# Stick-breaking attention: scores of two heads on the two halves of the array's rows, and a new order of score, turn and gather

## The chip, the cores and the metric

One Trainium2 chip, one core of it. The metric is the device time of the whole program in microseconds (us), smaller is better. The kernel before takes 2886.84 us (median of three runs, 2885.94 to 2888.79). The profiled execution, from which all rows below come, took 2888.11 us and has a span of 2886.3 us from its first to its last instruction.

## The reference, cut to what matters

The reference is one decoder block over 2048 positions: an input projection, a state-space mixer, stick-breaking attention with 8 heads of 64 elements, an output product, cross attention, and an MLP. The change touches the stick-breaking attention alone:

```
logits = einsum('bqhd,bkhd->bhqk', q, k) * scale        # 64 elements per head
mask = key_pos < q_pos
log_beta = log_sigmoid(logits)
log_1m_beta = where(mask, log_sigmoid(-logits), 0)
after = reverse cumsum over keys of log_1m_beta, less log_1m_beta
w = where(mask, exp(log_beta + after), 0)
out = einsum('bhqk,bkhd->bqhd', w, v)
```

The kernel does it as products: sigmoid(z) times the running product of sigmoid(-z) over the keys behind it. All data are float32. q and k of each head lie in device memory as two parts of 64 rows, a rounded part (hi) and what the rounding left (lo), so that q = hi + lo and k = hi + lo.

## The kernel before, in words

`stick_breaking` works on two heads at a time, in four steps (s). Within a step there are 16 blocks of 128 query positions (i). A block's keys are all keys up to its own, in tiles of 128, and `attention_units` cuts them into units of 1 to 4 tiles (128 to 512 keys), from the last keys to the first. A slot is one unit of one head; the slots alternate between the two heads (a = 0, 1), so a pair of slots, even and odd, is the same unit of both heads. There are 4 x 40 x 2 = 320 slots, or 160 pairs. The first unit of each block (`first`) holds the diagonal tile and is masked there.

Each slot m goes through these hands, each engine in its own written order:

- **score(m)** on TensorE (lines 957 to 982). The stationary operand is q2, 128 rows: q's hi part on the upper 64, its lo part on the lower 64. Line 976 multiplies it with k2_hi (k's hi part, stored twice, on both halves of the rows) and line 977 with k2_lo (likewise). That is two products of 128 rows for each slot, four in all for a pair, each as wide as the unit; a unit that crosses key 1024 is cut there in two segments. Line 979 adds the mask on the diagonal tile. The result is in one of five PSUM banks (`z_ps`, ZS = 5). TensorE waits until slot m - 5, which had the bank before, was scanned.
- **sigmoids(m)** on ScalarE: line 886 writes sigmoid(z) to `on`, line 887 writes sigmoid(-z) over z.
- **scan(m)** on VectorE (line 921): the running product into `left`.
- **w(m)** on GpSimd (line 873): `on` times `left`. Ring of WS buffers.
- **turn(m)** on TensorE (line 991): one transpose for each tile, into one of two PSUM banks (`wt_ps`). It waits (line 988) until the bank's last user, the slot two before, was copied out.
- **copies(m)**: the transposed weights from PSUM to `wt`. Slots with m % 3 != 2 are copied by ScalarE (line 895), the others by VectorE (line 932). Every slot has at most four tiles, so a slot is one such group.
- **gather(m)** on TensorE for a pair (line 1010): values times weights, with 64 columns of the array for each of the two heads; each tile and head gives two instructions in the trace.
- **copy_y** on VectorE (line 943), once for two finished blocks.

The order on each engine is set by lags, in slots. TensorE's loop over m issues score(m + 4), then turn(m - 3), and after every second m gather(m - 8) for the pair m - 8, m - 7. ScalarE's loop issues sigmoids(m), then copies(m - 7). VectorE's issues copy_y(m - 9), copies(m - 5), scan(m). Nothing else orders them but semaphores. SyncE loads q, k and v a half step ahead, and stores the result.

Of the kernel before, what the change touches and what calls it, by code (L numbers as in the profile page):

```python
# [7 lines left out]
F32 = mybir.dt.float32  # L8
F32R = mybir.dt.float32r
# [6 lines left out]
P = 128  # L16
BANK = 512
D_MODEL = 1024
SEQ = 2048
# [5 lines left out]
HEAD = 64  # L25
# [10 lines left out]
DMA = 16  # L36
# [683 lines left out]
def stick_breaking(nc, q_dram, k_dram, v_dram, yt_dram, ahead):  # L720

    BLOCKS = SEQ // P
    HALF = SEQ // 2
# [4 lines left out]
    SLOTS = [(s, a, *u) for s in range(STEPS) for u in UNITS for a in range(2)]  # L728
    N = len(SLOTS)
    PER_STEP = N // STEPS  # L730
    ZS, ONS, WS, WTS = 5, 6, 6, 8
    LEAD, TURN_LAG, ACT_LAG, DVE_LAG, GATHER_LAG, Y_LAG = 4, 3, 7, 5, 7, 9
    with ExitStack() as ctx:
        def sb(name, shape, dt=F32):
            return ctx.enter_context(nc.sbuf_tensor("a_" + name, shape, dt))

        sem = ctx.enter_context(semaphores(nc, "a_"))

        q2 = [sb(f"q2_{a}", [P, SEQ], F32R) for a in range(2)]
        k2_hi = [[sb(f"k2_hi{a}{r}", [P, HALF], F32R) for r in range(3)] for a in range(2)]  # L740
        k2_lo = [[sb(f"k2_lo{a}{r}", [P, HALF], F32R) for r in range(3)] for a in range(2)]
        v = [[sb(f"v{a}{r}", [P, BLOCKS * HEAD // 2]) for r in range(3)] for a in range(2)]
        ident = sb("ident", [P, P])
        ident16 = sb("ident16", [P, P], BF16)
        never16 = sb("never16", [P, P], BF16)
# [6 lines left out]
        z_ps = [ctx.enter_context(nc.psum_tensor(f"a_ps_z{b}", [P, WIDE], F32)) for b in range(ZS)]  # L752
# [6 lines left out]
        q_loaded = [sem(f"q_loaded{h}") for h in range(2)]  # L759
        k_loaded = [sem(f"k_loaded{h}") for h in range(2)]  # L760
        v_loaded = [sem(f"v_loaded{h}") for h in range(2)]
        begin_loaded = [sem(f"begin_loaded{a}") for a in range(2)]
        y_stored = [sem(f"y_stored{part}") for part in range(4)]
        scored = sem("scored")
# [20 lines left out]
        def wait(eng, of, count):  # L785
            if count > 0:
                eng.wait_ge(of, count)
# [4 lines left out]
        def wait_copied(eng, g):  # L792

            wait(eng, copied_a, acts_before[g + 1])
            wait(eng, copied_d, g + 1 - acts_before[g + 1])

        def load_begin(eng, a, cols, done_q, done_k):

            eng.dma_start(q2[a][:, cols].bitcast(F32), q_dram[a, :, cols]).then_inc(done_q, DMA)
            for dst, part in ((k2_hi[a][0], 0), (k2_lo[a][0], 1)):  # L800
                for copy in range(2):
                    eng.dma_start(dst[copy * HEAD:(copy + 1) * HEAD, cols].bitcast(F32),
                                  k_dram[a, part * HEAD:(part + 1) * HEAD, cols]).then_inc(done_k, DMA)

        @block.sync
        def _(sp):
            def load_half(s, half):
                cols = slice(half * HALF, (half + 1) * HALF)
                r = (2 * s + half) % 3
                if s > 0:  # L810
                    scores_of_q = final_slot[(s - 1) * BLOCKS + (BLOCKS // 2 - 1 if half == 0 else BLOCKS - 1)] + 1
                    wait(sp, scored, scores_of_q)
                for a in range(2):
                    sp.dma_start(q2[a][:, cols].bitcast(F32), q_dram[2 * s + a, :, cols]).then_inc(q_loaded[half], DMA)
                step_out = s - 1 if half else s - 2
                wait(sp, scored, (step_out + 1) * PER_STEP)
                for a in range(2):
                    for dst, part in ((k2_hi[a][r], 0), (k2_lo[a][r], 1)):
                        for copy in range(2):
                            sp.dma_start(dst[copy * HEAD:(copy + 1) * HEAD, :].bitcast(F32),  # L820
                                         k_dram[2 * s + a, part * HEAD:(part + 1) * HEAD, cols]).then_inc(k_loaded[half], DMA)
                wait_gathered(sp, (step_out + 1) * PER_STEP)
                for a in range(2):
                    h = 2 * s + a
                    sp.dma_start(v[a][r][:, :].rearrange("p (i d) -> p i d", d=HEAD),
                                 v_dram[cols, h * HEAD:(h + 1) * HEAD].rearrange("(i p) d -> p i d", p=P)).then_inc(v_loaded[half], DMA)

            def store_half(s, half):
                for part in (2 * half, 2 * half + 1):
                    wait(sp, y_copied, (s * BLOCKS + (part + 1) * 4) // 2)  # L830
                    sp.dma_start(yt_dram[s * P:(s + 1) * P, part * BANK:(part + 1) * BANK], yt[:, part, :]
                                 ).then_inc(y_stored[part], DMA)

            load_begin(sp, 0, slice(0, BANK), begin_loaded[0], begin_loaded[0])
            for a in range(2):
                sp.dma_start(v[a][0][:, :].rearrange("p (i d) -> p i d", d=HEAD),
                             v_dram[0:HALF, a * HEAD:(a + 1) * HEAD].rearrange("(i p) d -> p i d", p=P)
                             ).then_inc(v_loaded[0], DMA)
            for a in range(2):
                load_begin(sp, a, slice(BANK, HALF), q_loaded[0], k_loaded[0])  # L840
            load_half(0, 1)
            ahead.load_first(sp, ahead_loaded)
            for s in range(STEPS):
                store_half(s, 0)
                if s + 1 < STEPS:
                    load_half(s + 1, 0)
                    load_half(s + 1, 1)
                else:
                    sp.wait_ge(y_stored[0], STEPS * DMA)
                    ahead.load_ys(sp, yt_dram, ahead_loaded)  # L850
                store_half(s, 1)
            sp.wait_ge(ahead_loaded, ahead.FIRST_LOADS * DMA)
            for part in range(4):
                sp.wait_ge(y_stored[part], STEPS * DMA)
# [99 lines left out]
        def _(pe):  # L954
            pe.wait_ge(constants, 5)

            def score(m):

                s, a, i, k0, k1, first, last = SLOTS[m]
                if s == 0 and i == 0:  # L960
                    pe.wait_ge(begin_loaded[a], 5 * DMA)
                elif i == (BANK // P if s == 0 else 0) or i == BLOCKS // 2 and first:
                    half = i // (BLOCKS // 2)
                    pe.wait_ge(q_loaded[half], (s + 1) * 2 * DMA)
                    pe.wait_ge(k_loaded[half], (s + 1) * 8 * DMA)
                wait(pe, scanned, m - ZS + 1)
                c0 = k0
                while c0 < k1:
                    c1 = min(c0 + BANK - (c0 - k0) % BANK, k1, (c0 // HALF + 1) * HALF)
                    r = (2 * s + c0 // HALF) % 3  # L970
                    cols = slice(c0 % HALF, c0 % HALF + c1 - c0)
                    out = z_ps[m % ZS][:, c0 - k0:c1 - k0]
                    diagonal = first and c1 == k1
                    opens = (c0 - k0) % BANK == 0
                    closes = c1 == k1 or (c1 - k0) % BANK == 0
                    pe.matmul(out, q2[a][:, i * P:(i + 1) * P], k2_hi[a][r][:, cols], start=opens, stop=False)  # L976
                    mm = pe.matmul(out, q2[a][:, i * P:(i + 1) * P], k2_lo[a][r][:, cols], start=False, stop=closes and not diagonal)
                    if diagonal:
                        mm = pe.matmul(z_ps[m % ZS][:, k1 - P - k0:k1 - k0], ident16[:, :], never16[:, :],  # L979
                                       start=False, stop=True)  # L980
                    c0 = c1
                mm.then_inc(scored, 1)

            def turn(m):
                pe.wait_ge(weighed, m + 1)
                for g in range(first_group[m], first_group[m + 1]):
                    _, t0, n = groups[g]
                    if g >= 2:
                        wait_copied(pe, g - 2)
                    for t in range(n):  # L990
                        mm = pe.transpose(wt_ps[g % 2][:, t * P:(t + 1) * P], w[m % WS][:, (t0 + t) * P:(t0 + t + 1) * P],  # L991
                                          ident[:, :])
                    mm.then_inc(turned, 1)
# [17 lines left out]
                                       wt[(m + a) % WTS][:, t, :], start=(first and t == 0), stop=(last and t == tiles - 1))  # L1011
                mm.then_inc(pairs_gathered, 1)

            for m in range(LEAD):
                score(m)
            for m in range(N + GATHER_LAG):
                if m + LEAD < N:
                    score(m + LEAD)
                if TURN_LAG <= m < N + TURN_LAG:
                    turn(m - TURN_LAG)  # L1020
                if m > GATHER_LAG and (m - GATHER_LAG) % 2:
                    gather(m - GATHER_LAG - 1)


def ssm_scan(nc, small, scan, u_dram, y_dram, mem, g_mem, w_kv, g_q, g_k, kt_dram, mv_dram):
# [1142 lines left out]
class UpInputs:  # L2168
# [4 lines left out]
    SLOTS = 4  # L2173
# [1244 lines left out]
```

## Time and profile before

| what | value |
|---|---|
| median of the runs | 2886.84 us |
| profiled execution: time, span | 2888.11 us, 2886.3 us |
| attention, first score product to last gather (within the span) | 596.5 us to 1040.4 us |
| of the whole span: PE, DVE, ACT, POOL busy | 94%, 64%, 47%, 32% |

PE is TensorE's matmuls, PEld its weight loads, DVE VectorE, ACT ScalarE, POOL GpSimd. Matmuls are pipelined: a row's duration goes on after the next one has started, so the cost of one is read from the difference of two starts, and not from its duration. The same holds in smaller measure for ACT, whose next instruction starts some 0.1 us before the last one's end.

### The profile page before, as it was taken

Reading aid. Unit: us, or ns where it says so; the run is one execution under the profiler, and the core shown is the slowest. Engines: PE = TensorE matmul, PEld = TensorE weight load, DVE = VectorE, ACT = ScalarE, POOL = GpSimd, SP = SyncE. Lnnn points to the kernel's source line nnn. Section 1 sums busy time; section 2 is a strip of 40 time slices with the busy share of each in tenths; the row PEclk is TensorE's granted clock in tenths of the full one; section 3 lists DMA queues with packets and bytes.
Section 4 is the critical chain, followed back from the end, with each engine's and each line's share of the span. In section 5 each row is a group of like instructions: output and inputs, shape, how many; then the busy total and the mean of one; then the engine's idle time right before and its main releaser. Section 6 shows DMA issues by size and latency. Waiting matters only on the chain. (4 is left out here: it accounts for less than half of the span.)

```text
span 2886.3 us, 43692 instructions
## 1 busy us (share of the span) xinstructions
PE 2721.2 (94%) x14835; PEld 2232.6 (77%) x14835; DVE 1854.6 (64%) x2821; ACT 1369.5 (47%) x2508; POOL 925.4 (32%) x839
## 2 busy tenths in 40 slices
PE   6999978979999989998999899999999999999998
PEld 5888874757777768876888688877888787878787
DVE  5343458958998975545666856565556758584853
ACT  4222225668888863323445555565555424242421
POOL 0010101746766732300000132242333344344442
PEclk9999988989999989998999999999999999999999
DMA  5433345283333133341322243325444465646554
GB/s 172 109 84 94 80 110 104 65 209 79 74 77 86 42 106 103 118 172 66 110 100 105 98 133 128 112 96 171 154 133 146 112 154 120 159 97 169 99 116 85
DMA packets 291144, 328.23 MB, mean 114 GB/s; under 512 B 113816, under 2 KB 220320, under 8 KB 290720
## 3 DMA queue, kind: packets, MB, share of 16 engines
q1 hardware_dynamic: 276704, 291.96, 33.9%
q0 software_dynamic: 13824, 33.56, 7.9%
q8 instruction: 83, 1.36, 0.2%
q10 hardware_dynamic: 464, 0.79, 0.1%
q14 instruction: 69, 0.57, 0.1%
HBM read 206.57 MB, written 126.88 MB: 116 GB/s over the span
## 5 line engine op out<-in xcount | busy, mean ns | idle before, releaser
L3329 PE MATMUL f_ps_bank<-f_big,h_wv 128*128 128x512 f32 x1280 | 503.2, 393 | 26.9 <-DVE f_big L3175 17.6
L3330 PE MATMUL f_ps_bank<-f_big,h_wv 128*128 128x512 f32 x1280 | 500.6, 391 | 0.0
L3331 PE MATMUL f_ps_bank<-f_big,h_wv 128*128 128x512 f32 x1280 | 500.3, 391 | 0.0
L873 POOL TENSOR_TENSOR a_w<-a_on,a_left 128x512 f32<-128x512 f32 (+3 forms) x320 | 304.2, 956 | 143.8 <-DVE a_left L921 131.8
L3015 POOL TENSOR_TENSOR h_w_sum<-w_raw 128x512 f32<-128x512 f32 x63 | 90.9, 1443 | 729.0 <-DMA w_raw<-in_w_up 453.4
L3072 ACT ACTIVATE h_wv<-h_w_sum 128x512 fp32r<-128x512 f32 x252 | 159.0, 631 | 345.7 <-PE f_ps_bank L3331 342.4
L3329 PEld LDWEIGHTS f_ps_bank<-f_big,h_wv 128*128 128x128 f32 x1280 | 241.7, 189 | 84.1 <-issue 28.9
L3331 PEld LDWEIGHTS f_ps_bank<-f_big,h_wv 128*128 128x128 f32 x1280 | 241.8, 189 | 50.7
L3171 DVE TENSOR_TENSOR h_wv<-w_raw,h_wv 128x512 fp32r<-128x512 f32 x189 | 177.9, 942 | 159.9 <-ACT h_wv L3072 155.8
L3330 PEld LDWEIGHTS f_ps_bank<-f_big,h_wv 128*128 128x128 f32 x1280 | 241.9, 189 | 49.8
L3072 ACT ACTIVATE h_wv<-w_raw 128x512 fp32r<-128x512 f32 x189 | 118.7, 630 | 198.0 <-PE f_ps_bank L3331 178.2
L921 DVE TENSOR_TENSOR_SCAN a_left<-a_ps_z,a_left,a_one 128x384 f32<-128x384 f32 (+2 forms) x192 | 202.6, 1096 | 0.0
L3330 PE MATMUL f_ps_bank<-hv_rest,h_wv 128*128 128x512 f32 x512 | 199.3, 389 | 0.0
L886 ACT ACTIVATE a_on<-a_ps_z 128x512 f32<-128x512 f32 (+3 forms) x320 | 171.0, 534 | 58.5 <-PE a_ps_z L979 35.9
L3171 DVE TENSOR_TENSOR h_wv<-h_w_sum,h_wv 128x512 fp32r<-128x512 f32 x252 | 186.1, 738 | 5.3 <-ACT h_wv L3072 1.5
L976 PE MATMUL a_ps_z<-a_k_hi,a_q 128*128 128x512 f32 (+3 forms) x368 | 155.2, 428 | 19.0 <-DMA a_k_lo<-k 14.5
L991 PE MATMUL a_ps_wt<-a_ident,a_w 128*128 128x128 f32 x1088 | 172.3, 274 | 0.2 <-DVE a_wt L932 0.2
L887 ACT ACTIVATE a_ps_z<-a_ps_z 128x512 f32<-128x512 f32 (+3 forms) x320 | 172.5, 539 | 0.0
L646 PE MATMUL p_acc<-p_w_hi,p_ht_hi 128*128 128x512 f32 x384 | 153.5, 400 | 3.6 <-DVE p_w_lo L542 3.6
L424 POOL TENSOR_TENSOR p_qn<-p_qn,p_gq_row 128x512 f32<-128x512 f32 x32 | 41.0, 1293 | 360.6 <-DVE p_qn L560 360.6
L1010 PE MATMUL a_ps_y<-a_wt,a_v 128*64 128x128 f32 x2176 | 153.7, 280 | 0.0
L648 PE MATMUL p_acc<-p_w_hi,p_ht_lo 128*128 128x512 f32 x384 | 151.0, 393 | 0.0
(430 smaller groups left out, 6323.3 us busy)
## 6 DMA issues: line engine op xcount, KB each, us to landing
w_raw<-in_w_up SPq DMA_DIRECT2D x32, 1024.0 KB, 6.7
a<-h_xr SPq DMA_DIRECT2D x128, 256.0 KB, 3.4
w_raw<-a SPq DMA_DIRECT2D x32, 1024.0 KB, 5.2
h_raw<-in_w_down SPq DMA_DIRECT2D x32, 512.0 KB, 6.6
out<-h_xr POOLq DMA_DIRECT2D x64, 256.0 KB, 4.4
out<-h_xr POOLq DMA_DIRECT2D x32, 512.0 KB, 5.6
early<-in_x SPq DMA_DIRECT2D x16, 512.0 KB, 4.6
q<-p_raw SPq DMA_DIRECT2D x64, 128.0 KB, 2.5
```

Source lines behind the costliest of these rows:

```text
L873: pool.tensor_tensor(w[m % WS][:, 0:k1 - k0], on[m % ONS][:, 0:k1 - k0], left[a][i % 2][:, at + k0 + 1:at + k1 + 1], ALU.mult).then_inc(we ...
L886: act.activation(on[m % ONS][:, 0:k1 - k0], z, ACT.Sigmoid, scale=SCALE).then_inc(sig_on, 1)
L887: act.activation(z, z, ACT.Sigmoid, scale=-SCALE).then_inc(sig_off, 1)
L921: dve.tensor_tensor_scan(left[a][i % 2][:, at + k0:at + k1][:, ::-1], z_ps[m % ZS][:, 0:k1 - k0][:, ::-1], one[:, 0:1].to_broadcast([P, k1 ...
L976: pe.matmul(out, q2[a][:, i * P:(i + 1) * P], k2_hi[a][r][:, cols], start=opens, stop=False)
L991: mm = pe.transpose(wt_ps[g % 2][:, t * P:(t + 1) * P], w[m % WS][:, (t0 + t) * P:(t0 + t + 1) * P], ident[:, :])
L1010: mm = pe.matmul(y_ps[a * HEAD:(a + 1) * HEAD, i % 2 * P:(i % 2 + 1) * P], v[a][(2 * s + half) % 3][:, cols], wt[(m + a) % WTS][:, t, :], ...
L3072: act.activation(wv(i, 0), W_SRC[i], ACT.Copy).then_inc(w_high.sem, 1)
L3171: dve.tensor_tensor(wv(i, 1), W_SRC[i], wv(i, 0).bitcast(F32), ALU.subtract).then_inc(w_low.sem, 1)
L3329: pe.matmul(o, wv(i, 0)[:, k, :], hv(i, 0)[:, k, :], start=(k == 0), stop=False)
L3330: pe.matmul(o, wv(i, 0)[:, k, :], hv(i, 1)[:, k, :], start=False, stop=False)
L3331: mm = pe.matmul(o, wv(i, 1)[:, k, :], hv(i, 0)[:, k, :], start=False, stop=(k == KH - 1))
```

## The change

q and k are stored once: `q_hi`, `q_lo`, `k_hi`, `k_lo` have head 0 on the upper 64 rows and head 1 on the lower 64. A score call is for a pair of slots. It makes three products for each head, hi x hi, lo x hi and hi x lo (the product lo x lo, which the kernel before had, is left out), each with 64 rows, the two heads' in turn, into two PSUM banks. The lags and the rings of buffers are changed, and gathers come for two pairs in a row.

```
-    ZS, ONS, WS, WTS = 5, 6, 6, 8
-    LEAD, TURN_LAG, ACT_LAG, DVE_LAG, GATHER_LAG, Y_LAG = 4, 3, 7, 5, 7, 9
+    ZS, ONS, WS, WTS = 5, 6, 8, 12
+    LEAD, TURN_LAG, ACT_LAG, DVE_LAG, GATHER_LAG, Y_LAG = 4, 4, 8, 6, 11, 11
+    BATCH = 4
...
-        q2 = [sb(f"q2_{a}", [P, SEQ], F32R) for a in range(2)]
-        k2_hi = [[sb(f"k2_hi{a}{r}", [P, HALF], F32R) for r in range(3)] for a in range(2)]
-        k2_lo = [[sb(f"k2_lo{a}{r}", [P, HALF], F32R) for r in range(3)] for a in range(2)]
+        q_hi, q_lo = [sb(f"q_{part}", [P, SEQ], F32R) for part in ("hi", "lo")]
+        k_hi, k_lo = [[sb(f"k_{part}{r}", [P, HALF], F32R) for r in range(3)] for part in ("hi", "lo")]
...
+        def load_q(eng, step, a, cols, done):
+            for part, dst in enumerate((q_hi, q_lo)):
+                eng.dma_start(dst[a * HEAD:(a + 1) * HEAD, cols].bitcast(F32),
+                              q_dram[2 * step + a, part * HEAD:(part + 1) * HEAD, cols]).then_inc(done, DMA)
+        def load_k(eng, step, a, r, to, cols, done):
+            for part, dst in enumerate((k_hi[r], k_lo[r])):
+                eng.dma_start(dst[a * HEAD:(a + 1) * HEAD, to].bitcast(F32),
+                              k_dram[2 * step + a, part * HEAD:(part + 1) * HEAD, cols]).then_inc(done, DMA)
...
-                wait(pe, scanned, m - ZS + 1)
+                wait(pe, scanned, m + 1 - ZS + 1)
+                rows = slice(i * P, (i + 1) * P)
+                bank = [z_ps[(m + a) % ZS] for a in range(2)]
+                ends = [(c0, c1) for c0, c1 in ((k0, min(k1, HALF)), (max(k0, HALF), k1)) if c0 < c1]
+                for c0, c1 in ends:
...
-                    pe.matmul(out, q2[a][:, i * P:(i + 1) * P], k2_hi[a][r][:, cols], start=opens, stop=False)
-                    mm = pe.matmul(out, q2[a][:, i * P:(i + 1) * P], k2_lo[a][r][:, cols], start=False, stop=closes and not diagonal)
...
+                    terms = ((q_hi, k_hi[r]), (q_lo, k_hi[r]), (q_hi, k_lo[r]))
+                    for n, (q, k) in enumerate(terms):
+                        for a in range(2):
+                            head = slice(a * HEAD, (a + 1) * HEAD)
+                            mm = pe.matmul(bank[a][:, c0 - k0:c1 - k0], q[head, rows], k[head, cols],
+                                           start=(c0 == k0 and n == 0), stop=(c1 == k1 and n == 2 and not first))
+                            if c1 == k1 and n == 2 and not first:
+                                mm.then_inc(scored, 1)
+                if first:
+                    for a in range(2):
+                        pe.matmul(bank[a][:, k1 - P - k0:k1 - k0], ident16[:, :], never16[:, :],
+                                  start=False, stop=True).then_inc(scored, 1)
...
-            for m in range(LEAD):
+            for m in range(0, LEAD, 2):
                 score(m)
-            for m in range(N + GATHER_LAG):
+            for m in range(0, N + GATHER_LAG + 1, 2):
                 if m + LEAD < N:
                     score(m + LEAD)
-                if TURN_LAG <= m < N + TURN_LAG:
-                    turn(m - TURN_LAG)
-                if m > GATHER_LAG and (m - GATHER_LAG) % 2:
-                    gather(m - GATHER_LAG - 1)
+                if 0 <= m + 1 - TURN_LAG < N:
+                    turn(m + 1 - TURN_LAG)
+                if 0 <= m + 2 - TURN_LAG < N:
+                    turn(m + 2 - TURN_LAG)
+                done = m + 1 - GATHER_LAG
+                if 0 <= done < N and done % BATCH == 0:
+                    for n in range(done, done + BATCH, 2):
+                        gather(n)
```

So TensorE's loop over even m is now: score of slots m + 4 and m + 5, turn(m - 3), turn(m - 2), and in every second round the gathers of slots m - 10 to m - 7. ScalarE's order is sigmoids(m), copies(m - 8); VectorE's is copy_y(m - 11), copies(m - 6), scan(m). The number of q and k transfers for a half step falls from 2 of 128 rows and 8 of 64 rows to 8 of 64 rows.

## Rows read from the trace of the kernel before

**Rows 1.** Busy time by stage: PE, PEld, DVE, ACT, POOL, clock, DMA share, GB/s.
```profile
620.00:1020.00 400.00, 400.00 (x3799) 317.35 (x3799) 360.60 (x422) 354.47 (x786) 280.52 (x294) 1.00 0.32 82
```
**Rows 2.** Waits from 620 to 1020 us: total us, times, longest.
```profile
DVE a_wt L932 <- PE a_ps_wt L991: 25.4, 34, 2.2
ACT a_on L886 <- PE a_ps_z L979: 23.7, 47, 1.0
ACT a_on L886 <- PE a_ps_z L977: 19.0, 47, 0.7
```
**Rows 3.** TensorE's matmuls in order: start us, us (from start to last end), what.
```profile
904.77 0.34 PE L977 MATMUL a_ps_z<-a_k_lo,a_q 128*128 128x384 f32 x1
...
905.85 0.60 PE L991 MATMUL a_ps_wt<-a_ident,a_w 128*128 128x128 f32 x4
906.38 1.09 PE L1010 MATMUL a_ps_y<-a_wt,a_v 128*64 128x128 f32 x16
907.40 0.50 PE L976 MATMUL a_ps_z<-a_k_hi,a_q 128*128 128x512 f32 x1
907.73 0.40 PE L977 MATMUL a_ps_z<-a_k_lo,a_q 128*128 128x512 f32 x1
907.97 0.49 PE L991 MATMUL a_ps_wt<-a_ident,a_w 128*128 128x128 f32 x3
...
908.48 0.34 PE L977 MATMUL a_ps_z<-a_k_lo,a_q 128*128 128x384 f32 x1
908.65 0.49 PE L991 MATMUL a_ps_wt<-a_ident,a_w 128*128 128x128 f32 x3
909.07 0.88 PE L1010 MATMUL a_ps_y<-a_wt,a_v 128*64 128x128 f32 x12
909.88 0.44 PE L976 MATMUL a_ps_z<-a_k_hi,a_q 128*128 128x384 f32 x1
```
**Rows 4.** TensorE's weight loads in the same stretch.
```profile
907.40 0.19 PEld L976 LDWEIGHTS a_ps_z<-a_k_hi,a_q 128*128 128x128 f32 x1 [0.17 <-issue]
907.51 0.19 PEld L977 LDWEIGHTS a_ps_z<-a_k_lo,a_q 128*128 128x128 f32 x1
```
**Rows 5.** ScalarE in order, two stretches.
```profile
905.14 0.60 ACT L886 ACTIVATE a_on<-a_ps_z 128x512 f32<-128x512 f32 x1 [0.31 <-PE a_ps_z L977]
905.64 0.59 ACT L887 ACTIVATE a_ps_z<-a_ps_z 128x512 f32<-128x512 f32 x1
906.16 0.59 ACT L895 ACTIVATE a_wt<-a_ps_wt 128x512 f32<-128x512 f32 x1
906.63 0.60 ACT L886 ACTIVATE a_on<-a_ps_z 128x512 f32<-128x512 f32 x1
...
956.33 0.48 ACT L895 ACTIVATE a_wt<-a_ps_wt 128x384 f32<-128x384 f32 x1
956.70 0.49 ACT L886 ACTIVATE a_on<-a_ps_z 128x384 f32<-128x384 f32 x1
957.06 0.50 ACT L887 ACTIVATE a_ps_z<-a_ps_z 128x384 f32<-128x384 f32 x1
957.47 0.50 ACT L895 ACTIVATE a_wt<-a_ps_wt 128x384 f32<-128x384 f32 x1
```
**Rows 6.** A masked slot: last mask product, ScalarE's start.
```profile
1022.08 0.23 PE L979 MATMUL a_ps_z<-a_never,a_ident 128*128 128x128 bf16 x1
...
1022.35 0.60 ACT L886 ACTIVATE a_on<-a_ps_z 128x512 f32<-128x512 f32 x1 [0.83 <-PE a_ps_z L979]
```
**Rows 7.** Groups by shape over the whole attention: ScalarE's off sigmoid, TensorE's products.
```profile
L887 ACT ACTIVATE a_ps_z<-a_ps_z 128x512 f32<-128x512 f32 x160 | 96.7, 604 | 0.0
L887 ACT ACTIVATE a_ps_z<-a_ps_z 128x384 f32<-128x384 f32 x136 | 67.4, 496 | 0.0
...
L991 PE MATMUL a_ps_wt<-a_ident,a_w 128*128 128x128 f32 x1088 | 172.3, 274 | 0.2 <-DVE a_wt L932 0.2
L1010 PE MATMUL a_ps_y<-a_wt,a_v 128*64 128x128 f32 x2176 | 153.7, 280 | 0.0
```

More of the change, by code:

```diff
@@ L795, in wait_copied @@
             wait(eng, copied_d, g + 1 - acts_before[g + 1])
-        def load_begin(eng, a, cols, done_q, done_k):
[L799 to L803, printed above, removed]
+        def load_q(eng, step, a, cols, done):
[6 more added lines that the diff above has]
+                              k_dram[2 * step + a, part * HEAD:(part + 1) * HEAD, cols]).then_inc(done, DMA)
+        def load_begin(eng, a, cols, done_q, done_k):
+            load_q(eng, 0, a, cols, done_q)
+            load_k(eng, 0, a, 0, cols, cols, done_k)
         @block.sync
@@ L813, in load_half @@
                 for a in range(2):
-                    sp.dma_start(q2[a][:, cols].bitcast(F32), q_dram[2 * s + a, :, cols]).then_inc(q_loaded[half], DMA)
+                    load_q(sp, s, a, cols, q_loaded[half])
                 step_out = s - 1 if half else s - 2
@@ L817, in load_half @@
                 for a in range(2):
[L818 to L821, printed above, removed]
+                    load_k(sp, s, a, r, slice(0, HALF), cols, k_loaded[half])
                 wait_gathered(sp, (step_out + 1) * PER_STEP)
@@ L957, in score @@
             def score(m):
-                s, a, i, k0, k1, first, last = SLOTS[m]
+                s, _, i, k0, k1, first, last = SLOTS[m]
                 if s == 0 and i == 0:
-                    pe.wait_ge(begin_loaded[a], 5 * DMA)
+                    for a in range(2):
+                        pe.wait_ge(begin_loaded[a], 4 * DMA)
                 elif i == (BANK // P if s == 0 else 0) or i == BLOCKS // 2 and first:
                     half = i // (BLOCKS // 2)
-                    pe.wait_ge(q_loaded[half], (s + 1) * 2 * DMA)
-                    pe.wait_ge(k_loaded[half], (s + 1) * 8 * DMA)
@@ L966, in score @@
-                wait(pe, scanned, m - ZS + 1)
-                c0 = k0
-                while c0 < k1:
-                    c1 = min(c0 + BANK - (c0 - k0) % BANK, k1, (c0 // HALF + 1) * HALF)
+                    pe.wait_ge(q_loaded[half], (s + 1) * 4 * DMA)
+                    pe.wait_ge(k_loaded[half], (s + 1) * 4 * DMA)
+                wait(pe, scanned, m + 1 - ZS + 1)
+                rows = slice(i * P, (i + 1) * P)
+                bank = [z_ps[(m + a) % ZS] for a in range(2)]
+                ends = [(c0, c1) for c0, c1 in ((k0, min(k1, HALF)), (max(k0, HALF), k1)) if c0 < c1]
@@ L970, in score @@
+                for c0, c1 in ends:
                     r = (2 * s + c0 // HALF) % 3
                     cols = slice(c0 % HALF, c0 % HALF + c1 - c0)
[L972 to L975, printed above, removed]
-                    pe.matmul(out, q2[a][:, i * P:(i + 1) * P], k2_hi[a][r][:, cols], start=opens, stop=False)
-                    mm = pe.matmul(out, q2[a][:, i * P:(i + 1) * P], k2_lo[a][r][:, cols], start=False, stop=closes and not diagonal)
@@ L978, in score @@
[L978 to L982, printed above, removed]
+                    terms = ((q_hi, k_hi[r]), (q_lo, k_hi[r]), (q_hi, k_lo[r]))
[6 more added lines that the diff above has]
+                                mm.then_inc(scored, 1)
@@ L984, in turn @@
+                if first:
+                    for a in range(2):
+                        pe.matmul(bank[a][:, k1 - P - k0:k1 - k0], ident16[:, :], never16[:, :],
+                                  start=False, stop=True).then_inc(scored, 1)
             def turn(m):
```

## The prediction

> **What bounds the kernel now.** I read the stage table first: from 620 to 1020 us, the steady part of the attention, TensorE is busy for all 400.00 us at a granted clock of 1.00, VectorE for 360.60, ScalarE for 354.47, GpSimd for 280.52 [rows 1]. The waits agree: VectorE and ScalarE wait for TensorE's transposes and scores, 25.4 + 23.7 + 19.0 us [rows 2], and TensorE's transposes waited 0.2 us for a copy in the whole attention [rows 7]. So TensorE's written order sets the end of this stage, and VectorE is 10% behind it: a faster TensorE could bring the stage down to 361/400 of its time at most. The attention has 736 score products, 128 masks, 1088 transposes and 2176 gather products, 4128 in all; 3799 of TensorE's records fall into the 400 us [rows 1, 7], so the 160 pairs cost 400 x 4128/3799 = 435 us of steady time, 2.72 us a pair. Nothing outside the attention is changed. From the units: 80 pairs are 4 tiles wide, 68 are 3, 8 are 2 and 4 are 1 (half of 160, 136, 16 and 8 slots; the first two counts stand in [rows 7]).
>
> **Prices on TensorE**, from differences of starts [rows 3]. A score product with its load hidden: 0.24 us at 512 columns (907.73 to 907.97), 0.17 at 384 (908.48 to 908.65). A load of 128 columns: 0.11 (907.40 to 907.51 [rows 4]); it is bare after a change of the array's shape, and hence L976 at 907.40 takes 0.33. A transpose: 0.11 (0.60 for four, 0.49 for three). From the last transpose to a gather's load: 908.65 + 2 x 0.11 = 908.87 to 909.07, 0.20, that is 0.09 more than a transpose. The gather of a pair to the next score's load: 1.02 at 4 tiles (906.38 to 907.40), 0.81 at 3 (909.07 to 909.88), so 0.0525 for one more gather product; two of them (both heads) take 0.105, as one transpose does, so the two column halves run side by side. A pair of 4 tiles before: 2 x (0.33 + 0.24) + (0.33 + 0.03) + (0.33 + 0.20) + 1.02 = 3.05; of 3 tiles 2 x (0.26 + 0.17) + 0.25 + 0.42 + 0.81 = 2.34. 80 x 3.05 + 68 x 2.34 + 12 x 1.5 + 128 masks x 0.07 + 5 for cut units = 435, the measured sum, so the prices hold.
>
> **Part 1, scores in three terms of 64 rows.** No row shows products on row halves. Bounds: the two heads' products side by side, so a term costs 0.24 or 0.17 for both, or one after the other, double. The nearest rows are the gathers on column halves, and they are side by side; I take that. A pair's scores then stream for 3 x 0.24 = 0.72 in place of 4 x 0.24, or 3 x 0.17. The loads: both at once (0.11) or one after the other (0.22). The gather's pairs of loads keep up with 0.105 a pair, so I take 0.11. What it adds: scores now have another shape than the transposes, so each pair has two changes with a bare load, and the gather two more in every second round. Bounds of a change: 0 to 0.2, taken 0.09 as in [rows 3].
> The Trainium skill, "TensorEngine Tiling (Array Packing)", section "Key Properties", says that tiles run loads and matmuls in parallel and that changing the tiling mode drains the array. The trace agrees with both on the column side (0.105 for two products, 0.20 in place of 0.11); for rows no run before shows it.
>
> **Part 2, gathers for two pairs in a row** take away one change into and out of the gather in two pairs, about 0.15 a pair. TensorE's work alone is then, for 4 tiles: load 0.11 + 0.72 + change 0.09 = 0.92; load 0.11 + 7 x 0.11 + 0.20 = 1.08, so 2.00; gather (1.02 + 16 x 0.0525)/2 = 0.93; in all 2.93 against 3.05. For 3 tiles: 1.57 + 0.72 = 2.29 against 2.34. Over all pairs 234 + 156 + 18 + 13 = 421 against 435. The change as a whole is worth 14 us of TensorE's time, if nothing waits.
>
> **Part 3, the lags; here I expect the loss.** Turn of slot m - 2 writes into a PSUM bank that slot m - 4 had, and waits for its copy. With ACT_LAG 8, ScalarE makes the copy of m - 4 only after the sigmoids of m + 4. TensorE issues the scores of m + 4 in this same round, just ahead of the turns. So in each round in which ScalarE copies the even slot, TensorE must go through: scores, two sigmoids, one copy, second turn. Before, the turn of m - 3 needed the copy behind the sigmoids of m + 2, scored two slots earlier, and the wait was 0.2 us in all. Behind the waiting turn stand, in order, the gathers and the next scores, so the whole pipeline waits: VectorE and GpSimd get no new slots.
> A round of 4 tiles: load 0.11, two terms 0.48, last term's start to ScalarE's start 0.44 (0.37 at 384 columns, 904.77 to 905.14 [rows 3, 5], and 0.07 more streaming), two sigmoids 1.02 (905.14 to 906.16), copy 0.59 [rows 5], signal back to TensorE 0.05 (no row; bounds 0 and 0.25, for the other direction takes 0.37 less 0.34 of the product's row = 0.03), turn 0.11 + 3 x 0.11 + 0.20 = 0.64. Sum 3.33. With 3 tiles: 0.11 + 0.34 + 0.37 + 0.77 + 0.49 + 0.05 + 0.53 = 2.66. Slots with m % 3 = 2 are VectorE's to copy, and its copy of m - 4 stands before the scan of m + 2, long done; this is one even slot of three, and such a round costs TensorE's own 2.00 or 1.57, and sometimes a late ScalarE: its work in it is 2 x 1.02 + 0.47, which ends at 1.03 + 2.51 = 3.54, while the next scores are there at 2.00 + 1.03, so 0.51 us late, unless gathers (1.86, or 1.44 at 3 tiles) lie between. Six pairs of 4 tiles: 4 x 3.33 + 2 x 2.00 + 3 x 1.86 + 0.51 = 23.4, or 3.90 a pair. Of 3 tiles: 4 x 2.66 + 2 x 1.57 + 3 x 1.44 + 0.34 = 18.4, or 3.07. In all 80 x 3.90 + 68 x 3.07 + 12 x 2.2 = 547. The 64 pairs with a mask: the mask comes after another change, and ScalarE starts 0.27 after it [rows 6], some 0.2 in the chain, 13 us; cut units 4 us. Together 564 us against 435: +129.
>
> **The rest.** The larger rings (WS 8, WTS 12) and lags of gather and copy_y cost nothing: a gather of slots up to m - 7 needs copies older than the one that the turn before it waited for, and the y copy of a finished block precedes a scan two rounds later. If that cover went, VectorE would be late by about one copy (0.49 [rows 5]) at 32 places, 16 us. q and k transfers fall from 10 to 8 in a half step and in bytes; the DMA share is 0.32 now [rows 1], and they go a half step ahead. Only the first pair waits for both heads' loads, with 2 transfers fewer in front: between -2 and +2 us, taken as 0.
> Sum: 2888.1 of the profiled execution + 129 = 3017; the median of the runs is 1.3 us under it, so **3016 us**.
>
> **Rivals.**
> A. The wait at the turn does not bind, and TensorE's own sum counts: 2888 - 14 = 2874. For it: the wait for copies is next to nothing now, and ScalarE has 11% to spare. Against it: the copy cannot precede sigmoids of slots that were not scored. It decides if the copy of m - 4 ends by 1.4 us after the round's start, where the second turn is due; I work it out at 2.6.
> B. The row halves don't run side by side, and the change doesn't do what it says: 80 x 0.72 + 68 x 0.51 + 4 = 97 us more, less some 5 as the even slot's last term comes before the odd one's: 3108. For it: no row shows two row halves. Against it: column halves do it.
> C. Products side by side, loads one after the other: 160 x 0.11 for the first, and terms under 0.22 wide become 0.22: 18 + 10 + 16 = 44 us, 3060. For it: a term of 3 tiles has 0.17 for two loads. Against it: the gather's rows. The Trainium skill, "TensorE: Matmul & The Clock Gate", section "LDWEIGHTS (loading the stationary operand)", says that a load of fewer rows takes as long as one of 128, its columns count; with the loads in turn that gives C's sum, and side by side mine.
> D. No net change (gains and waits cancel): it would need the stall of about 1 us in two rounds of three to shrink to 0.1.
>
> **How the numbers follow.** Mine 0.72, A 0.11, B 0.08, C 0.07, D 0.02. My own range: the signal back at 0 to 0.25 us gives -5 to +21 over 107 rounds, a change of shape at 0 to 0.2 gives -20 to +25, VectorE's rounds +-10: 2985 to 3060. To hold 8 in 10 it takes in C and B, and some of the way to A: 2960 to 3115. Less than 0.2% (6 us) is not told from no change. Faster 0.11 (A), same 0.02, slower 0.87.
>
> **What would show it.** Right: between the attention's two ends some 570 us in place of 444; TensorE idle for about 140 us of it, put down to ScalarE's copy (L895) at the transposes, some 1 us each in about 107 rounds, all of them at even slots; VectorE and ScalarE at some 70% busy; two scores' products of a term starting within some ns. Wrong: TensorE still at 100% there (A), a term's products 0.24 apart (B), its loads 0.11 apart (C), or a stall at scores for `scanned` or at gathers.

## The result: slower by 4.7%, 3023.12 us

The changed kernel takes 3023.12 us (median of four runs, 3020.43 to 3023.24) against 2887.05 us before (four runs). The ratio is 1.0467, 95% interval 1.0454 to 1.0480. The profiled execution took 3023.07 us with a span of 3021.3 us, 135.0 us more than before's 2886.3. All of it lies in the attention: from the first score product to the last gather it was 596.5 to 1040.4 us, 443.9 us, and is now 593.5 to 1172.2 us, 578.7 us. Of all runs below one stands apart: one of x6's ten took 8975.28 us, unexplained, and without it x6's median would be 2880.70 in place of 2880.82 us.

The stage table of the changed kernel, with the columns of [rows 1]: first its steady part, then the whole attention.

```profile
620.00:1150.00 530.00, 413.07 (x4172) 306.89 (x4170) 370.96 (x425) 355.66 (x790) 283.35 (x297) 0.97 0.19 47
593.50:1172.20 578.70, 453.92 (x4496) 337.05 (x4496) 397.13 (x457) 383.46 (x854) 304.25 (x320) 0.95 0.21 53
```

TensorE was busy for all 400 of 400 us [rows 1] and is now idle for 117 of 530. VectorE fell from 90% to 70%, ScalarE from 89% to 67%. No engine has taken TensorE's place as the bound: all of them wait, so the time is in a loop of waits.

The matmuls and ScalarE's instructions of one round of the changed kernel, columns as in [rows 3] and [rows 5]; x2 is the two heads' products:

```profile
901.32 0.50 PE L984 MATMUL a_ps_z<-a_k_hi,a_q_hi 64*128 64x512 f32 x2
901.65 0.40 PE L984 MATMUL a_ps_z<-a_k_hi,a_q_lo 64*128 64x512 f32 x2
901.89 0.40 PE L984 MATMUL a_ps_z<-a_k_lo,a_q_hi 64*128 64x512 f32 x2
902.22 0.28 PE L990 MATMUL a_ps_z<-a_never,a_ident 128*128 128x128 bf16 x2
902.34 0.50 PE L1000 MATMUL a_ps_wt<-a_ident,a_w 128*128 128x128 f32 x3
904.08 0.41 PE L1000 MATMUL a_ps_wt<-a_ident,a_w 128*128 128x128 f32 x2 [1.24 <-POOL a_w L879]
904.42 0.45 PE L984 MATMUL a_ps_z<-a_k_hi,a_q_hi 64*128 64x384 f32 x2
```
```profile
902.48 0.60 ACT L892 ACTIVATE a_on<-a_ps_z 128x512 f32<-128x512 f32 x1 [1.76 <-PE a_ps_z L990]
902.98 0.59 ACT L893 ACTIVATE a_ps_z<-a_ps_z 128x512 f32<-128x512 f32 x1
903.49 0.48 ACT L901 ACTIVATE a_wt<-a_ps_wt 128x384 f32<-128x384 f32 x1
903.86 0.59 ACT L892 ACTIVATE a_on<-a_ps_z 128x512 f32<-128x512 f32 x1
```

Read together they are the chain. It is the round of one even m: TensorE scores slots m + 4 and m + 5, then turns m - 3 (the first turn) and m - 2 (the second). The scores of the pair are made from 901.32. ScalarE, idle for 1.76 us until then, takes the even slot's two sigmoids (902.48, 902.98) and only then the old slot's copy, 903.49 to 903.97. The second turn, ready since 902.67, starts at 904.08, 1.24 us idle. The next scores come at 904.42, and a round of 3.1 us is over. The row names GpSimd's weights as what ended the wait. GpSimd's product for that slot, 256 keys wide, had been done before 898.7, so the label can't be right; the copy ends 0.11 us ahead of the start. This wait is all over the attention ("issue" is time for which the profile shows nothing that was waited for):

```profile
POOL a_w L879 <- DVE a_left L927: 213.8, 141, 7.5
ACT a_on L892 <- PE a_ps_z L990: 110.1, 60, 4.3
DVE a_wt L938 <- PE a_ps_wt L1000: 109.2, 81, 4.4
PEld a_ps_wt L1000 <- POOL a_w L879: 107.3, 105, 1.4
ACT a_on L892 <- PE a_ps_z L984: 78.4, 67, 3.7
PE a_ps_wt L1000 <- POOL a_w L879: 78.0, 84, 1.2
...
PE a_ps_wt L1000 <- issue: 40.2, 45, 1.2
```

TensorE's matmuls stood 78.0 + 40.2 us before transposes, where it was 0.2 us [rows 7]. Counted round by round on the timeline, whatever their label, the second turn has 106 waits, 103.7 us, and 104 of these end 0.08 to 0.12 us after the end of a copy by ScalarE. The first turn has 26 waits, 16.6 us, each of which ends as close behind such a copy.

### The profile page after: what moved, and what is told of

Same layout as the page of the kernel before. It is cut to its first block and busy times, and to the rows that moved or that the text cites. A ratio compares the mean times of both kernels' runs of the same rounds, so it can differ in the third digit from the quotient of the medians.

```text
span 3021.3 us, 44397 instructions
## 1 busy us (share of the span) xinstructions
PE 2737.4 (91%) x15203; PEld 2222.2 (74%) x15203; DVE 1854.8 (61%) x2821; ACT 1369.3 (45%) x2508; POOL 926.3 (31%) x839
## 5 line engine op out<-in xcount | busy, mean ns | idle before, releaser
L3184 DVE TENSOR_TENSOR h_wv<-w_raw,h_wv 128x512 fp32r<-128x512 f32 x189 | 171.8, 909 | 164.9 <-ACT h_wv L3085 160.6
L1000 PEld LDWEIGHTS a_ps_wt<-a_ident,a_w 128*128 128x128 f32 x1088 | 117.5, 143 | 172.6 <-POOL a_w L879 107.3
L647 PE MATMUL p_acc<-p_w_lo,p_ht_hi 128*128 128x512 f32 x384 | 150.6, 392 | 0.0
```

The source lines that it names most:

```text
L3184: dve.tensor_tensor(wv(i, 1), W_SRC[i], wv(i, 0).bitcast(F32), ALU.subtract).then_inc(w_low.sem, 1)
```

## The experiments

Twelve kernels ran, each beside runs of the kernel before on the same chip, whose median was 2886.29 to 2888.53 us; the ratios are to those. A difference between two kernels of different sets is good to some 2 us. The stage rows have the columns of [rows 1].

### x1 to x4: which edit makes the loss

x1 is the changed kernel with one number put back:

```
-    LEAD, TURN_LAG, ACT_LAG, ... = 4, 4, 8, 6, 11, 11
+    LEAD, TURN_LAG, ACT_LAG, ... = 4, 4, 7, 6, 11, 11
```

> The changed kernel with ACT_LAG 7 in place of 8, nothing else: ScalarE copies the even slot's transposed weights before the sigmoids of the scores that are issued in the same round. Theory (the chain score, two sigmoids, copy, second turn costs the time): the stall goes and TensorE's own sum is left, 2874 us, 2865 to 2890. Rival 1 (the loss is in the scores on row halves and their changes of shape): still 3010 to 3025. Rival 2 (the loss is the score's wait for both slots' scans, or VectorE): still above 2950.

Measured: 2899.85 us, ratio 1.0046 (1.0030 to 1.0063). The lag alone holds 123 of the 136 us. Rivals 1 and 2 of this run are out. But it is 26 us over the 2874 of TensorE's own sum and 10 above the range that I gave it, and slower than before, clear of the noise. Its steady part shows 25 us of idle TensorE still; on the timeline the attention has 51 waits at the second turn, 25.2 us, and 47 of them end 0.08 to 0.12 us after a copy by ScalarE:

```profile
620.00:1030.00 410.00, 384.70 (x4119) 293.04 (x4115) 360.62 (x418) 346.21 (x781) 279.19 (x292) 1.00 0.24 61
```

x2 is the kernel before with `ACT_LAG` 8 in place of 7.

> The kernel before with ACT_LAG 8 in place of 7, nothing else. Theory: the lag alone makes the loss, since in the old order the turn of m - 3 then needs the copy behind the sigmoids of m + 3, scored one slot earlier; two rounds of a 4-tile pair then take some 4.0 us where ScalarE copies, 3.05 elsewhere: +60 to +110 us, 2950 to 3000. Rivals 1 and 2: within 10 us of the kernel before, 2887.

Measured: 2980.62 us, 1.0329 (1.0312 to 1.0346). The lag makes the loss in the old kernel too, with the old scores and the old gathers, at the size worked out. TensorE is busy for 420 of its 490 steady us.

x3 keeps the lag at 8 and moves the even slots' copies:

```
-        by_act = [g % 3 != 2 for g in range(len(groups))]
+        by_act = [g % 2 == 1 for g in range(len(groups))]
```

> The changed kernel with ACT_LAG 8 kept, but VectorE copies all even slots (by_act = g % 2 == 1) in place of every third. Theory: the even slot's copy is no longer behind ScalarE's sigmoids, so the stall goes although the lag stays; VectorE gets 54 more copies of some 0.55 us, 30 us, and comes close to TensorE: 2875 to 2910. Rival 1: still 3010 or more. Rival 2 (VectorE is what is short): slower than 3020.

Measured: 2929.27 us, 1.0150 (1.0134 to 1.0167). 94 us of the loss go although the lag stays, which no rival without ScalarE's copy explains. It is 19 us above my range, and VectorE is not the bound: it is busy for 386.69 of 440 us, and TensorE still waits at transposes.

```profile
620.00:1060.00 440.00, 382.21 (x4126) 294.87 (x4125) 386.69 (x471) 329.79 (x737) 282.31 (x295) 1.00 0.23 57
```

The second turn, whose bank VectorE now empties, has 3.7 us of waits left, in 6 places. The first turn has 53.6 us in 71, and each of them ends 0.08 to 0.12 us after the end of a copy by ScalarE:

```profile
905.68 0.34 PE L984 MATMUL a_ps_z<-a_k_lo,a_q_hi 64*128 64x384 f32 x2
...
908.32 1.06 PE L1000 MATMUL a_ps_wt<-a_ident,a_w 128*128 128x128 f32 x8 [0.56 <-POOL a_w L879]
```
```profile
906.04 0.49 ACT L892 ACTIVATE a_on<-a_ps_z 128x384 f32<-128x384 f32 x1 [1.75 <-PE a_ps_z L984]
...
907.21 0.49 ACT L893 ACTIVATE a_ps_z<-a_ps_z 128x384 f32<-128x384 f32 x1
907.62 0.60 ACT L901 ACTIVATE a_wt<-a_ps_wt 128x512 f32<-128x512 f32 x1
```

It is a second chain of the same lag. The turn of m - 3 needs the copy of m - 5, which in x3 is always ScalarE's, and at `ACT_LAG` 8 that copy stands behind the sigmoids of m + 2 and m + 3, whose scores were made one round earlier: scores to 905.86, four sigmoids from 906.04, the copy at 907.62, the turn at 908.32. My expectation had only the even slots' copy. The changed kernel's 26 waits at the first turn are the same wait. No run has x3's copies with lag 7 or with one pair's gathers, so how much of it the batching makes is open.

x4 is x1 with `BATCH = 2` and `GATHER_LAG` 9: one pair's gathers in each round.

> As x1, with gathers of one pair in each round (BATCH 2, GATHER_LAG 9) in place of two pairs in every second. Theory: two more changes of shape in two pairs, 0.15 us a pair, 24 us more than x1: 2890 to 2905. If the batching is worth nothing: the time of x1. If the batching's long stretch without scores costs something: faster than x1.

Measured: 2877.41 us, 0.9971 (0.9958 to 0.9983), 0.3% faster than the kernel before and 22 us faster than x1. The sign of my batching step is wrong here. (The 24 us of the expectation are 160 pairs at the 0.15 us that the prediction names for batching; its own sum took 0.09 a pair, 14 us.) TensorE is busy for 388 of 390 us:

```profile
620.00:1010.00 390.00, 388.34 (x4117) 292.03 (x4118) 358.92 (x418) 349.15 (x779) 278.42 (x292) 1.00 0.25 64
```

### x5: why batching costs

x5 is x1 with `ACT_LAG` 6.

> The changed kernel with ACT_LAG 6 (BATCH 4 kept). x1 left TensorE idle for 25 us of 410. Theory S (the copy chain still has one slot of slack too few): one more slot frees it, 2860 to 2880. Theory B (the burst: ScalarE starves during the gathers of two pairs and then has more work per round than TensorE's short round of 2.0 us gives it time for, so a lag cannot help): 2890 to 2905, as x1.

Measured: 2880.72 us, 0.9981 (0.9971 to 0.9990). That is 19 us better than x1, so most of x1's stall was slack (S), but the time is 0.7 us above the range of S, and 11 us of 390 stay idle:

```profile
620.00:1010.00 390.00, 378.89 (x4084) 291.04 (x4082) 357.80 (x415) 342.33 (x775) 277.58 (x291) 1.00 0.25 63
```
```profile
ACT a_wt L901 <- PE a_ps_wt L1000: 42.1, 54, 1.9
```

ScalarE now waits 42.1 us for transposes: its copy of m - 2 stands behind the sigmoids of m + 4 and before those of m + 5, and needs a turn of this same round. Evidence for the burst is how long ScalarE waits for scores at lag 7: 41.6 + 21.8 = 63.4 us in x1's steady part and 28.5 + 10.2 = 38.7 in x4's, with one pair's gathers. That a round without gathers is too short for ScalarE and one with four slots' gathers too long is my reading of these; no run took it apart. Both theories held in part: at lags 6, 7 and 8 two pairs' gathers in a row cost 8, 22 and 21 us against one pair's (x10, x4 and x9).

### x6: are the row halves side by side?

```
-                    for n, (q, k) in enumerate(terms):
-                        for a in range(2):
+                    for a in range(2):
+                        for n, (q, k) in enumerate(terms):
```

> x4 (ACT_LAG 7, one pair's gathers a round) with the three products of head 0 issued before the three of head 1, so that neighbours use the same row half. If products on the two halves run side by side: a pair streams five terms in place of three (head 1's first beside head 0's last), 0.46 us at 4 tiles and 0.34 at 3, 60 to 65 us over x4's 2877: 2935 to 2945; up to 2975 if nothing overlaps. If they never ran side by side: 2877.

Measured: 2880.82 us, 0.9977 (0.9967 to 0.9987), 3 us over x4 and nowhere near 2935. From the first gather to the last it is 420.5 us against x4's 419.9. Read by my expectation that would say that they never ran side by side. The trace says the contrary:

```profile
900.57 0.45 PE L984 MATMUL a_ps_z<-a_k_hi,a_q_hi 64*128 64x384 f32 x2
900.85 0.34 PE L984 MATMUL a_ps_z<-a_k_hi,a_q_lo 64*128 64x384 f32 x2
901.03 0.34 PE L984 MATMUL a_ps_z<-a_k_lo,a_q_hi 64*128 64x384 f32 x2
```

Head 1's first product is recorded 10 ns after head 0's first, and not after its third, though it stands behind it in the program. Terms follow at 0.18 us, the streaming time of one product of 384 columns (0.17 in [rows 3]). So in this trace each half goes through its own products in order, and the order between the halves in the program makes no difference. The experiment as I designed it could not slow the halves down; what settles the question is the spacing: two products every 0.18 or 0.24 us, where a product of 128 rows takes the same alone.

### x7 and x8: what the scores are worth

x7 is the kernel before, its `score` and rings untouched, with x4's loop and lags (two calls of `score` a round). x8 is x4 with the old rings, `WS, WTS = 6, 8`.

> The kernel before, with its scores (two products of 128 rows a slot) and its rings, but x4's order (pairs, TURN_LAG 4, ACT_LAG 7, DVE_LAG 6, GATHER_LAG 9, Y_LAG 11, one pair's gathers a round). The scores on row halves save one term of 0.24 (0.17 at 3 tiles) a pair and pay a change of shape and a bare load, 0.20: nearly nothing is left, so this is within 5 us of x4, 2872 to 2882. Rival: the row halves bring x4's gain over the kernel before, and this takes 2885 to 2895.

> x4 with the rings of the kernel before (WS 6, WTS 8). Theory: the rings are long enough either way, 2877 within 3 us. Rival: the longer rings bring part of x4's gain, 2880 to 2890.

Measured: x7 2891.52 us, 1.0014 (1.0004 to 1.0024); x8 2878.43 us, 0.9969 (0.9959 to 0.9980). The rings are worth nothing, as expected. x7 and x8 differ in the scores alone, with their loads of q and k, and the new ones bring 13 us; I had said within 5, so the rival was right. The two traces share it out. Up to the first gather x7 takes 598.7 to 615.4 us, 16.7, and x8 595.3 to 608.1, 12.8; the rest to the last gather is 430.4 and 420.0. So 4 us come at the start, where x7 has a second stretch at half clock, 606.6 to 613.4, and x8 none, and 10 in the rest. Taken round by round from score to score (147 rounds, from 628.6 us in x7 and from 621.1 in x8), they differ by 10.4 us too, and 9.0 of these lie in the 56 rounds with a mask, 1.4 in the 91 without, and 2.9 in the 24 pairs cut at key 1024, some of which are masked too. A masked pair of 4 tiles, x7's and then x8's, up to its first transpose:

```profile
903.14 0.50 PE L977 MATMUL a_ps_z<-a_k_hi,a_q 128*128 128x512 f32 x1
903.48 0.40 PE L978 MATMUL a_ps_z<-a_k_lo,a_q 128*128 128x512 f32 x1
903.72 0.23 PE L980 MATMUL a_ps_z<-a_never,a_ident 128*128 128x128 bf16 x1
903.75 0.48 PE L977 MATMUL a_ps_z<-a_k_hi,a_q 128*128 128x512 f32 x1
...
904.38 0.94 PE L992 MATMUL a_ps_wt<-a_ident,a_w 128*128 128x128 f32 x7
```
```profile
899.67 0.49 PE L984 MATMUL a_ps_z<-a_k_hi,a_q_hi 64*128 64x512 f32 x2
...
900.56 0.29 PE L990 MATMUL a_ps_z<-a_never,a_ident 128*128 128x128 bf16 x2
900.69 1.04 PE L1000 MATMUL a_ps_wt<-a_ident,a_w 128*128 128x128 f32 x8
```

It takes 1.24 us before and 1.02 now. Behind the first head's mask the second head's first product took 0.32 us (903.75 to 904.07), the price with a bare load; the new scores come for both heads, and then both masks. The cut units have little of the gain.

### x9: the batching undone alone

x9 is the changed kernel with `ACT_LAG` 8 kept, `BATCH = 2` and `GATHER_LAG` 9.

> The changed kernel with ACT_LAG 8 kept and the gathers of one pair a round (BATCH 2, GATHER_LAG 9): the batching undone alone. Theory (each round in which ScalarE copies the even slot takes the chain of 3.33 us at 4 tiles and 2.66 at 3, and the gathers come behind it): six pairs of 4 tiles 4 x 3.33 + 2 x 2.00 + 6 x 1.02 = 23.4, of 3 tiles 18.6, against 23.4 and 18.4, so the time stays, 3018 to 3030. Rival: the batching feeds the stall here as it did at ACT_LAG 7 (22 us between x1 and x4), about 3000.

Measured: 3001.91 us, 1.0394 (1.0377 to 1.0412). The rival is right: batching costs 21 us here too. Its waits at the first turn, 16.6 us in the changed kernel, are 2.4 us here (7 waits), while those at the second turn are alike, 103.7 us in the changed kernel and 106.5 here. Another part is the clock. The last but one column is the granted clock: x9's steady part first, then from the changed kernel one of the nine stretches at half clock that lie behind 620 us, and the stretch behind it.

```profile
620.00:1130.00 510.00, 407.57 (x4142) 293.01 (x4143) 367.68 (x421) 354.18 (x783) 281.40 (x295) 1.00 0.20 49
```
```profile
905.70:909.10 3.40, 3.40 (x31) 3.07 (x31) 1.49 (x2) 1.50 (x5) 2.18 (x2) 0.51 0.02 5
909.10:912.50 3.40, 2.16 (x20) 1.32 (x16) 2.88 (x5) 1.92 (x5) 0.86 (x1) 0.99 0.20 77
```

Eight of the nine, 27.2 us, are in the steady part, 620 to 1150 us, and one begins at 1158.4; the expectation of x11 below counts nine in the steady part. The start is slower too: the changed kernel is at half clock from 602.0 to 619.0 us, x9 from 604.0 to 610.8. TensorE had worked in short pieces before the fall at 905.7: matmuls in 902.3 to 902.8, nothing until 904.08, and from 905.2 to 905.45 nothing again. What it then does at 1.2 GHz is two pairs' gathers, the longest work of all. The same 28 gather products in the changed kernel at half clock and in x1 at full:

```profile
906.41 3.07 PE L1019 MATMUL a_ps_y<-a_wt,a_v 128*64 128x128 f32 x28
```
```profile
902.48 1.75 PE L1019 MATMUL a_ps_y<-a_wt,a_v 128*64 128x128 f32 x28
```

### x11: the clock's share

x11 keeps the chain as long as it is and gives TensorE work while it waits:

```
+                    again = 3 if m % 2 and m > 8 and by_act[m - 1] else 1
-                    for t in range(n):
+                    for t in list(range(n)) * again:
                         mm = pe.transpose(wt_ps[g % 2][:, t * P:(t + 1) * P], ...
```

> The changed kernel, but in the rounds where the second turn waits for ScalarE's copy, the first turn's transposes are done three times (the same data into the same bank), so TensorE works for 0.66 to 0.88 us of a stall of 1.0 to 1.25 us. The copy chain is as long as before. The changed kernel has nine stretches at a granted clock of 0.5 in its steady part, 30.6 us; the kernel with one pair's gathers a round (x9) has none and is 21 us faster. Theory C (the idle time of TensorE lets the clock fall, and that costs up to half of 30.6 us): the clock stays at 1.00 and the time is 3008 to 3018. Theory N (the clock costs nothing that the stalls don't hide): 3020 to 3026. If the extra transposes come in the chain's way: over 3026.

Measured: 3011.41 us, 1.0436 (1.0419 to 1.0454), 12 us less than the changed kernel (9 by the two ratios) with 712 more transposes. The clock stays at 1.00, and at the start the half clock ends at 610.2 us:

```profile
620.00:1140.00 520.00, 474.68 (x4870) 371.82 (x4870) 371.60 (x425) 358.12 (x794) 285.48 (x298) 1.00 0.20 48
```

Theory C holds: some 12 us were the clock, the start included. Without them the time is 3011 us, and 9 us of batching's 21 are not the clock.

### x10 and x12: a faster version

x10 is x4 with `ACT_LAG` 6. x12 is the kernel before with `ACT_LAG` 6.

> x4 with ACT_LAG 6. x4 left TensorE idle for only 1.7 us of 390, so no lag can bring more than 2 us: 2874 to 2880. If ScalarE waiting for the transposes holds up its sigmoids: 2880 to 2890.

> The kernel before with ACT_LAG 6 in place of 7. x10 (2872.66) has that lag and the row halves. Before, TensorE is busy for all of 400 us of 400, so the lag can't bring anything: 2884 to 2890. Rival: the lag itself is what made x10 faster: 2878 to 2883.

Measured: x10 2872.66 us, 0.9943 (0.9927 to 0.9960); x12 2888.01 us, 0.9998 (0.9989 to 1.0008). x10 beats both kernels, by 16 us (0.6%) and by 150 us. TensorE is busy for 390.00 of 390 us in it. x12 shows that the lag alone does nothing in the old kernel, where TensorE has no room to fill. x10 came out 1 us below the range that I gave it, 5 us below x4; from the first gather to the last the two traces have 414.5 and 419.9 us. I had taken x4's 1.7 us of idle time for all that a lag can bring. But x10 gets 4166 products into 390 us and x4 4117, 1.2% fewer, which is 4.6 us: a product's recorded time goes on after the next could have started, so waits of a tenth of a microsecond are counted as busy.

## Why the prediction was right, and where not

- **What bounds the kernel.** Right for the kernel before, where TensorE filled 400 of 400 us; in the changed kernel no engine is over 78% busy.
- **Part 3, the chain at the second turn.** Right, in place, sign and size. Expected: rounds of 3.33 us at 4 tiles and 2.66 at 3, and 2.00 and 1.57 where VectorE copies. Measured behind 620 us, as means of the rounds without mask and gathers, sorted by the width of their scores: 3.20 (11 rounds) and 2.80 (9), and 2.10 (5) and 1.76 (7). Expected in all: +129 us, with some 1 us of idle time in 107 rounds, all at even slots; measured: 103.7 us in 106 waits at even slots, and, not expected, 16.6 us in 26 at odd ones, the wait that x3 shows by itself. With the clock held up, x11 gives 2888.53 + 122.9 us; the changed kernel's +136 is that and some 13 us of clock (12 by the medians as they are). x1 takes it away with the lag alone, x2 makes it in the old kernel, x3 takes most of it away without touching the lag. The idle time worked out, some 140 us in the attention, is 578.7 - 453.9 = 124.8 us.
- **What the lag alone is worth.** The prediction's two levels, 2874 without the wait and 3016 with it, are 142 us apart; measured are 123, 12 of them the clock. The level without the wait was set 26 us too low and the step too large. The forecast did not go through that level but from the length of the rounds, and so it stands; a forecast by the step would have owed its hit to luck.
- **The signal back, 0.05 us taken.** The copy's end to the transpose's start is 0.11 us in the round shown (903.97 to 904.08), and to the load 0.08; over all 106 waits the middle value is 0.10. Over 107 rounds that is some 5 us more than I had.
- **The granted clock.** Missing in the prediction. It cost some 12 us, more than what the forecast was short by (3016 against 3023); the rest of the sum is therefore some 5 us too high, and that the two partly cancel is luck.
- **Part 1, terms side by side, loads at once.** Right: 901.32, 901.65, 901.89 with two products each, loads within 3 ns of each other. Rivals B and C are out. The change of shape back to transposes is 901.89 + 0.24 to 902.22, 0.09, the value taken. Mis-sized: the term's worth in all. The sum gave the new scores a gain of nothing over the old ones; x7 against x8 gives 13 us, 9 of them in rounds with a mask and 4 at the start. Against the kernel before, the order in pairs and the new scores together bring 9 us (x8), where the sum without the batching has about nothing.
- **Part 2, gathers in pairs.** Wrong in sign. 14 us of TensorE's work were to be saved (0.15 us a pair in the words, 0.09 in the sum); measured is a loss of 8 us at lag 6 (x5, x10), 22 at lag 7 (x1, x4) and 21 at lag 8 (x9). The step that failed is that TensorE's sum counts alone: ScalarE's copies come later, and TensorE waits for them, by 25 us at lag 7 and at the first turn at lag 8. Of the 21 us some 12 are the clock.
- **The rest at nothing.** Right for the rings (x8). The order in pairs with the old scores costs 4 us (x7).
- **Rival A, 2874.** Its condition was made true in x1, and its number was missed by 26 us, 22 of them for the batching; without batching x4 gives 2877 and x10 2873. That these two meet 2874 is luck: its 14 us were to come from the batching, which loses, and the gain came from the scores, which were put at nothing.

The steps from before to after: order in pairs +4 (x7), new scores -13 (x8), batching +22 (x4 to x1), lag 7 to 8 +123 (x1 to the changed kernel), 136 us. They are neighbours in one row of kernels, so that they add up is no check, and in another order a step can have another size.

## What to carry to other kernels

When an order of work is changed from single units to pairs, look at every ring of two buffers: the wait is not on the lag alone but on what the copying engine must do ahead of that copy, and if one of those steps needs a result issued in the same round, the round becomes a chain through both engines. A lag one larger than needed cost 123 us here, nine times what the better matmuls gave. Look at both buffers: when the even slots' copies went to VectorE, TensorE still waited 53.6 us for the odd ones' (x3). Count batching not by the switches that it saves alone but also by what the next engine waits for during the burst. And where a wait's label and the times disagree, look for the event that always ends just ahead of it.

## What the runs showed of the hardware that was not expected

- Products on the two row halves start each in its own half's order: head 1's first product was recorded 10 ns after head 0's first although two others of head 0 stood between them in the program (x6), at 2881 against 2877 us. The Trainium skill ("TensorE: Matmul & The Clock Gate", section "Step-by-step: what each phase is for") has matmuls stay in program order; across the two halves this trace differs, and agrees with the Trainium skill, "TensorEngine Tiling (Array Packing)", section "Key Properties", that tiles operate independently.
- In the changed kernel TensorE, with no wait at its matmuls over 1.2 us behind 620 us, fell to a granted clock of 0.5 (1.2 GHz) in nine stretches, 30.6 us in all, and left it late at the start, at 619.0 us; together this cost some 12 us (x11). With one pair's gathers a round and waits of the same length (x9) it did not fall once behind 620 us, and neither did x1, x2 or x3. What makes the difference stays open.
- The wait of a transpose for a buffer carried GpSimd's name or none in the profile, where 104 of 106 such waits in the changed kernel ended 0.1 us behind a copy by ScalarE.
